# The last feed-forward's gate and up products: Strassen's seven half-size products in place of eight

## The reference, cut to what matters

```
def swiglu_2(a, w13, w2):
    gate, up = jnp.split(a @ w13, 2, axis=-1)
    return (jax.nn.silu(gate) * up) @ w2

f_lat = swiglu_2(modulate(h_lat, m_lat[3], m_lat[4]), ffn_w13[i], ffn_w2[i])
h_lat = layer_norm(DEEPNORM_ALPHA * h_lat + m_lat[5] * f_lat, ln_g[i, 1], ln_b[i, 1])
```

## Time and profile before

| | |
|---|---|
| median of 3 runs | 2859.49 us |
| profiled execution: span from first to last instruction | 2854.2 us |
| what lies around the span (median less span) | 5.3 us |
| PE / DVE / ACT / POOL busy over the span | 99% / 55% / 38% / 19% |
| f4, pairs of parts 2 and 3 (16 pairs) | 87.0 us for each 8 |

### The profile page before, as it was taken

The page is one execution under the profiler, slowest core; times in us unless marked ns, Lnnn a source line. Parts: engine busy times, 40 slices in busy tenths (PEclk is TensorE's granted clock), DMA queues, the critical chain, the costliest instruction groups (busy, mean ns, idle before and its releaser), DMA issues.

```text
span 2854.2 us, 40607 instructions
## 1 busy us (share of the span) xinstructions
PE 2821.6 (99%) x16234; PEld 2449.4 (86%) x16234; DVE 1576.0 (55%) x2738; ACT 1098.0 (38%) x1884; POOL 545.1 (19%) x287
## 2 busy tenths in 40 slices
PE   9999999999999999999999999999999999999998
PEld 8888897988889888888888988888897778988888
DVE  6656588757585543534446743533565636633344
ACT  5322258633234541423324722112235546532222
POOL 2333200033331101111111011111112322122220
PEclk9999999999999999999999999999999999999999
DMA  5544322235553201110211132322422121133231
GB/s 191 166 157 162 119 86 73 68 125 178 164 165 100 75 30 59 52 64 33 67 52 52 45 106 89 118 87 95 137 62 98 54 76 65 53 111 103 96 96 38
DMA packets 85005, 268.85 MB, mean 94 GB/s; under 512 B 9040, under 2 KB 16592, under 8 KB 84432
## 3 DMA queue, kind: packets, MB, share of 16 engines
q1 hardware_dynamic: 84816, 266.25, 28.5%
HBM read 262.54 MB, written 2.10 MB: 93 GB/s over the span
## 4 chain that ended last, share of the span: by engine, by line
PE 95%; DVE 3%; ACT 1%; issue 1%; DMA 0%; SPq 0%; DVEq 0%; ACTq 0%
PE ps L1762 30%; PE ps L1763 30%; PE ps L1764 30%; PE ps L2021 1%; PE ps L2005 1%; PE ps L1994 1%; DMA t_x<-in_x 0%; PE ps L1885 0%; DVE t_m L2403 0%; PE ps L1877 0%; PE ps L1936 0%; DVE t_wlo L2383 0%; PE ps L1893 0%; PE ps L1949 0%; DVE t_m L2465 0%
## 5 line engine op out<-in xcount | busy, mean ns | idle before, releaser
L1762 PE MATMUL ps<-t_h,t_whi 128*128 128x512 f32 (+1 forms) x2320 | 807.0, 348 | 3.5 <-DVE t_wlo L2377 1.3
L1763 PE MATMUL ps<-t_h,t_wlo 128*128 128x512 f32 (+1 forms) x2320 | 802.3, 346 | 0.0
L1764 PE MATMUL ps<-t_h,t_whi 128*128 128x512 f32 (+1 forms) x2320 | 801.6, 346 | 0.0
L2896 POOL TENSOR_TENSOR t_wlo<-t_raw,t_whi 128x1024 fp32r<-128x1024 f32 (+3 forms) x144 | 342.4, 2377 | 1500.7 <-ACT t_whi L2059 1500.7
L2059 ACT CAST t_whi<-t_raw 128x1024 fp32r<-128x1024 f32 (+3 forms) x320 | 320.7, 1003 | 632.3 <-PE ps L1764 592.5
L1762 PEld LDWEIGHTS ps<-t_h,t_whi 128*128 128x128 f32 x2320 | 439.3, 189 | 63.7 <-issue 8.2
L1763 PEld LDWEIGHTS ps<-t_h,t_wlo 128*128 128x128 f32 x2320 | 439.4, 189 | 54.4 <-issue 1.2
L1764 PEld LDWEIGHTS ps<-t_h,t_whi 128*128 128x128 f32 x2320 | 439.1, 189 | 53.9
L1762 PE MATMUL ps<-t_hid,t_whi 128*128 128x256 f32 (+1 forms) x1298 | 421.1, 324 | 0.6 <-DVE t_hid L2530 0.6
L1763 PE MATMUL ps<-t_hid,t_wlo 128*128 128x256 f32 (+1 forms) x1298 | 418.9, 323 | 0.0
L1764 PE MATMUL ps<-t_hid,t_whi 128*128 128x256 f32 (+1 forms) x1298 | 418.3, 322 | 0.0
(11 more groups left out here) (306 smaller groups left out, 4118.5 us busy)
## 6 DMA issues: line engine op xcount, KB each, us to landing
t_raw<-in_gu SPq DMA_DIRECT2D x174, 512.0 KB, 3.3
t_raw<-in_ada SPq DMA_DIRECT2D x96, 512.0 KB, 3.3
t_raw<-in_dn SPq DMA_DIRECT2D x52, 512.0 KB, 3.7
t_raw<-in_dn SPq DMA_DIRECT2D x24, 384.0 KB, 3.2
t_raw<-in_ret_v SPq DMA_DIRECT2D x16, 512.0 KB, 3.3
t_raw<-in_ret_qk SPq DMA_DIRECT2D x16, 512.0 KB, 4.2
t_raw<-in_ret_g SPq DMA_DIRECT2D x16, 512.0 KB, 3.2
t_raw<-in_ret_o SPq DMA_DIRECT2D x16, 512.0 KB, 3.8
```

Source lines behind the costliest of these rows:

```text
L1762: e.matmul(out, whi, xlo, start=first, stop=False, skip_group_check=shared)
L1763: e.matmul(out, wlo, xhi, start=False, stop=False, skip_group_check=shared)
L1764: return e.matmul(out, whi, xhi, start=False, stop=last, skip_group_check=shared)
L2896: e.tensor_tensor(m.block(1, it.slot, n), m.raw(it), m.block(0, it.slot, n), ALU.subtract).then_inc(*S["lo_pool"].of(j))
```

## The change

For 19 of f4's 22 pairs (all but the first three) gate and up are computed together by the Winograd form of Strassen's scheme. The pair is a 2 x 2 matrix of quarters: A11, A12 are gate's weights for the lower and the upper 512 channels, A21, A22 are up's; B11, B12, B21, B22 are the activations, lower or upper channels by first or second 256 tokens. In place of 8 products of quarters there are 7:

- P1 = A11 B11, P2 = A12 B21, P3 = S4 B22, P4 = A22 T4, P5 = S1 T1, P6 = S2 T2, P7 = S3 T3
- sums of weights: S1 = A21 + A22, S2 = S1 - A11 (written as A22 - S3), S3 = A11 - A21, S4 = A12 - S2
- sums of activations, once for all pairs: T1 = B12 - B11, T3 = B22 - B12, T2 = B22 - T1, T4 = B21 - T2 in the kernel's signs.

Each of the seven is 4 steps x 3 matmuls of 256 tokens, with 128 x 512 of weights. PE's order is P1, P2, P6, P5, P7, P3, P4. P6, P7 and P4 go on in P1's PSUM bank after P1, and P3 in P5's; before such a bank is added to, its content is copied to SBUF by ACT (`snap`), or, ahead of P4, taken by DVE (`seven_add` of C22). DVE makes the four results: C11 = P1 + P2, C12 and C22 by one addition each from a copy and a bank, C21 is the bank itself.

POOL makes S3, S1 and S4 of every pair in place in the ring (`wadd`), DVE makes S2 into a spare corner of TMP. ACT copies the seven quarters to hi; POOL writes lo of A12 and S3, DVE of the other five. WHI and WLO are used as eight half slots. A pair's two loads (gate's and up's block) keep their places in the ring until their last sums are split: the first until S3 and S4 are, the second until S1 and A22 are. The activations' sums are made in four chunks c = 0 to 3: POOL adds hi and lo of four quarters (`t_full`), DVE makes T1, T3, T2, T4 one from another (`t_add`), ACT and DVE split them (`t_hi`, `t_lo`); the next chunk's `t_full` waits for this chunk's `t_lo`.

```diff
+QUADS = ("A11", "A12", "S2", "S1", "S3", "S4", "A22")
+HALF = 20
+FULLS = {"T1": 0, "T3": 1, "T4": 2, "T2": 3}
+WADD_POOL = ("S1", "S3", "S4")
+WLO_POOL = ("A12", "S3")
...
+        if slot < NH and known:
+            spare.extend((HALF + 2 * slot + h, after) for h in range(2))
...
+    def assign_half(slot, after):
+
+        j = take_coming()
+        where[j] = slot
+        (pid, srcs), q = known[j]
+        low[j] = "lo_pool" if q in WLO_POOL else "lo_dve"
+        if q == "A11":
+            for which in range(2):
+                put("load", pid=pid, which=which, src=srcs[which])
+        put("prep", j=j, slot=slot, after=after, lo=low[j], q=q, pid=pid)
+        put("prep_lo", j=j)
+        if q == "A12":
+            for name in ("S3", "S1", "S2", "S4"):
+                put("wadd", pid=pid, q=name, old=state["pair"])
+            state["pair"] = pid
...
+                if halves:
+                    for s in range(segs[-1][0] // 256 + 1):
+                        force_tokens(s * 256, 256)
+                    turned_sums(f, ver, halves)
+            if halves:
+                gates, last_h = seven_products(f, ver, gu, [(pi, k, c0 + k) for k in range(size - len(specs) // 2, size)], halves, gates, over_hid, pitch)
...
+    def turned_sums(f, ver, halves):
+
+        after = halves["after"]()
+        for c in range(DC // 2):
+            put("t_full", f=f, ver=ver, c=c, n=halves["n"], after=after)
+            put("t_add", f=f, c=c, n=halves["n"])
+            put("t_hi", f=f, c=c, n=halves["n"], after=after)
+            put("t_lo", f=f, c=c, n=halves["n"])
...
+            banks = {"P1": bank(), "P2": bank(), "P5": bank()}
+            banks.update(P6=banks["P1"], P7=banks["P1"], P4=banks["P1"], P3=banks["P5"])
...
+            product("P1", "A11", "B11", seat(banks["P1"], "drain_dve", (*key, "up", 0)))
+            s1, keys1 = snap("P1")
+            product("P2", "A12", "B21", seat(banks["P2"], "drain_dve", (*key, "C11")))
+            gate1 = gate_slot()
+            add("C11", s1, ids["P2"], banks["P2"], gate1, gates[gate1])
+            free(keys1, ("drain_dve", (*key, "C11")))
+            put("seven_silu", key=(*key, "C11"), slot=gate1, n=n)
+            gates[gate1] = [("drain_dve", (*key, "up", 0))]
+            product("P6", "S2", "T2", [("snap", (*key, "P1"))])
+            s2, keys2 = snap("P6")
+            product("P5", "S1", "T1", seat(banks["P5"], "drain_dve", (*key, "C12")))
+            s5, keys5 = snap("P5")
+            product("P7", "S3", "T3", [("snap", (*key, "P6"))])
+            add("C22", s5, ids["P7"], banks["P7"], None)
+            product("P3", "S4", "B22", [("snap", (*key, "P5"))])
+            gate2 = gate_slot()
+            add("C12", s2, ids["P3"], banks["P3"], gate2, gates[gate2])
+            free(keys2, ("drain_dve", (*key, "C12")))
+            put("seven_silu", key=(*key, "C12"), slot=gate2, n=n)
+            gates[gate2] = [("drain_dve", (*key, "up", 1))]
+            last = product("P4", "A22", "T4", [("drain_dve", (*key, "C22"))])
+            up(0, gate1, None)
+            up(1, gate2, s5)
+            free(keys5, ("drain_dve", (*key, "up", 1)))
...
+                elif old.kind == "load":
+                    for j, lo in old.last:
+                        w.wait_ge("hi", j)
+                        w.wait_ge(lo, j)
...
+    def seven(it):
+        out = m.PS[:, it.bank, 0:it.n]
+        for k in range(4):
+            if k:
+                yield
+            if it.x[0] == "T":
+                w.wait_ge("t_lo", (it.f, it.x, k))
+            else:
+                wait_h(it.ver, (int(it.x[1]) - 1) * 4 + k, (int(it.x[2]) - 1) * it.n, it.n)
+            if k == 0:
+                w.wait_ge(it.lo, it.w)
+                wait_all(it.before)
+            done = products(out, m.weight(0, it.slot, k * P, P), m.weight(1, it.slot, k * P, P), m.factor(it, 0, k), m.factor(it, 1, k),
+                            it.first and k == 0, k == 3, True)
...
+    def wadd(it):
+        if it.q not in WADD_POOL:
+            r1, r2 = it.raws
+            w.wait_ge("wadd_pool", (it.pid, "S3"))
+            w.wait_ge(f"d_ring{r2 % NR}", r2)
+            wait_all(it.taken)
+            e.tensor_tensor(m.quad(r2, "S2"), m.quad(r2, "A22"), m.quad(r1, "S3"), ALU.subtract).then_inc(*S["wadd_dve"].of((it.pid, it.q)))
...
+    def t_add(it):
+        f11, f12, f21, f22 = (m.full(i, it.n) for i in range(4))
+        w.wait_ge("t_sum", (it.f, it.c))
+        e.tensor_tensor(f11, f12, f11, ALU.subtract).then_inc(*S["t_full"].of((it.f, "T1", it.c)))
+        w.wait_ge("t_full", (it.f, "T1", it.c))
+        e.tensor_tensor(f12, f22, f12, ALU.subtract).then_inc(*S["t_full"].of((it.f, "T3", it.c)))
+        w.wait_ge("t_full", (it.f, "T3", it.c))
+        e.tensor_tensor(f22, f22, f11, ALU.subtract).then_inc(*S["t_full"].of((it.f, "T2", it.c)))
+        w.wait_ge("t_full", (it.f, "T2", it.c))
+        e.tensor_tensor(f21, f21, f22, ALU.subtract).then_inc(*S["t_full"].of((it.f, "T4", it.c)))
...
+        r1, r2 = it.raws
+        q11, q12, q21, q22 = m.quad(r1, "A11"), m.quad(r1, "A12"), m.quad(r2, "A21"), m.quad(r2, "A22")
+        if it.q == "S3":
+            w.wait_ge(f"d_ring{r2 % NR}", r2)
+            w.wait_ge("hi", it.pid)
+            w.wait_ge(it.lows["A11"], it.pid)
+            done = e.tensor_tensor(q11, q11, q21, ALU.subtract)
+        elif it.q == "S1":
+            w.wait_ge("wadd_pool", (it.pid, "S3"))
+            done = e.tensor_tensor(q21, q21, q22, ALU.add)
+        else:
+            w.wait_ge("wadd_dve", (it.pid, "S2"))
+            w.wait_ge("hi", it.pid + 1)
+            w.wait_ge(it.lows["A12"], it.pid + 1)
+            done = e.tensor_tensor(q12, q12, m.quad(r1, "S2"), ALU.subtract)
+        done.then_inc(*S["wadd_pool"].of((it.pid, it.q)))
...
+    def t_full(it):
+        n = it.n
+        wait_all(it.after)
+        if it.c:
+            for t in ("T1", "T2", "T3", "T4"):
+                w.wait_ge("t_lo", (it.f, t, it.c - 1))
+        for i in range(4):
+            c, t0 = it.c + i // 2 * 4, i % 2 * n
+            for s in halves(t0, n):
+                w.wait_ge("h_lo", (it.ver, c, s))
+            done = e.tensor_tensor(m.full(i, n), m.h(0, c, t0, n), m.h(1, c, t0, n), ALU.add)
```

231 lines of the change are left out of this document (203 added, 28 removed).

## The result

The changed kernel takes 2882.0 us (median of 4 runs, 2879.0 to 2885.6), the kernel before, run beside it, 2858.8 us (2857.9 to 2861.3). The ratio is 1.0081 with a 95% interval of 1.0068 to 1.0093: 23 us slower, where 2875 us and a range of 2850 to 2892 were forecast. The profiled execution took 2885.6 us, its span is 2883.8 us, 29.6 us more than before's 2854.2. That is more than the 23.2 us between the medians. The profiled execution of the changed kernel was the slowest of its four. That of the kernel before, at 2854.2 us and some 2 us for start and end (1.8 here), is 2 us shorter than any of the three timed ones (2858.0 to 2861.3).

The account below looks back on a forecast made before the run. PE's columns alone were taken to bound the last feed-forward. -15.2 + 22.8 + 6 + 1 + 1 = +15.6 us took the 2854.2 us span to 2869.8; 5.3 us around it made 2875, range 2850 to 2892.

Parts of the forecast that it names:

- waits at weights, 19 pairs: PE's stalls ahead of P7: 13 pairs at 1.5 us and 6 at about 0.5, +22.8 us.
- around it: Instructions the planner moves elsewhere in the kernel: 0, within 2 us either way.
- PE's part: PE's matmuls in f4's pairs: 10.88 us falls to 10.08, 0.80 us less a pair, 15.2 us in 19 pairs.
- The closed chain: POOL's and DVE's turns at SBUF plus the next pair's second load: 11.6 us a pair, PE waiting 1.5 before P7.
- count of pairs: Which of the 19 pairs stall: 13 at 1.5 us and 6 at about 0.5.
- Rival 3: C11 and C22 late too, PE waiting twice a pair: 12.2 us in all 19, +32 us, 2891; chance 12%.
- Rival 4: Weight loads bind, so no PE time saved: 11.0 us a pair, same stalls, 2890; 4% with the rest.
- Rival 1: Weights in stock hide the lag: pairs of 10.1 to 10.5 us, near 2855; chance 25%.
- The first pair: PE waits at P6 for the fourth chunk of T2, whose sums stand behind weights on POOL: 6 us.
- the upper bound I had given (12): First pair's wait if the fourth chunk's POOL sums and DVE instructions each wait out another turn: 12 us.
- The clock: TensorE's clock may halve after the first pair's pause: 0 to 3 us, 1 taken.
- The handovers: Each part's last pair to its down products, waiting for the hidden block's splits: 1 us for three parts.

Follow-up runs that it names:

- e3: Changed kernel with ACT's copy of P6's bank moved ahead of the hi of S2; 2886.5 us, ratio 1.0097 to the kernel before.
- e9: Changed kernel with an unused 512 KB transfer issued ahead of every second load of a pair, from the third pair on; 2908.0 us, ratio 1.0171 to before.
- e5: Changed kernel with POOL's three sums of weights cut to 8 of their 512 columns; 2866.1 us, ratio 1.0027 to the kernel before.
- e1: Changed kernel with a fourth place in the ring of raw weights from the third pair on; 2886.8 us, ratio 1.0104 to the kernel before.
- e4: Changed kernel with ACT's copy of P6 ahead of the hi of S2 and DVE's C22 ahead of the lo of S1; 2886.0 us, ratio 1.0101 to before.
- e6: Changed kernel with eight products again in part 1's three pairs, seven only in parts 2 and 3; 2870.8 us, ratio 1.0046 to the kernel before.
- e8: Changed kernel with the lo of down weights soon after a seven-product block made on DVE, not POOL; 2881.5 us, ratio 1.0081 to before.
- e2: Changed kernel with the lo of A12 and S3 made on DVE, not POOL; 2877.2 us, ratio 1.0066 to the kernel before.

## Why the prediction was right, and where it was off

The direction and the mechanism of the pairs were right. The sum was short by more than its time shows. In spans it gave +15.6 us, and the profiled execution has +29.6: 14 us short, most of it in two terms. That the forecast of 2875 missed the median of 2882 by only 7 is luck: the sum added 5.3 us to get from a span to the median, and for the changed kernel the median lies 1.8 us under the profiled span (2882.0 and 2883.8). Against the sum's own terms, in us of the profiled executions:

| term | forecast | measured |
|---|---|---|
| PE's columns, 19 pairs | -15.2 | -15.2 by 0.120 a matmul |
| waits at weights, 19 pairs | +22.8 | +20.8 in parts 2 and 3, 1.7 in part 1 |
| first pair, activations' sums | +6 | +9.15 in two gaps |
| clock at the first pair | +1 | +3.8, the rest of part 1 |
| handovers to down products | +1 | +8.8 |
| around it | 0 | +0.6 |

The measured 20.8 are the 7.96 us by which parts 2 and 3 grew and the 16 x 0.80 that PE saved in them; 19.8 of them stand as gaps, 1.0 is 16 times the 0.06 us by which a pair's matmuls took longer than 10.08. The 3.8 are what is left of part 1's 12.17 by 3 x 0.80, 9.15 and the gaps of 0.98 and 0.69.

**PE's part** was right to a tenth: the 84 matmuls of a pair take 10.14 us (11.70 less 1.56), which saves 0.74 us a pair and not 0.80.

**The closed chain** was right, and to a tenth: 11.6 to 11.7 forecast and 11.70 measured, the gap 1.5 and 1.56, ahead of P7 and behind ACT's copy, S3 waiting for the load. e3 shows that the wait is the round's and not the copy's, e9 that the load is in it, e5 that POOL's sums are 1.06 us of it. What the prediction didn't have is the second round through PE and DVE's queue, which e1 laid bare: the chain named is the longest of several, and none of its links that was taken away gave its own length back. Its count of pairs was off and did no harm: 13 pairs at 1.5 and 6 at 0.5 were forecast, ten have 1.56, the last pair of part 3 still 1.39, and the first ones of parts 2 and 3 none.

**Rival 3's sum** was too low: 12.2 us in all 19 pairs are 19 x 2.12 = 40 us of stalls and not 36, so that it comes to 2895, over the stated range. No pair of parts 2 and 3 came near it (11.70 at most). Rival 4's was too low as well: 11.0 us a pair with the same stalls is 2893, not 2890.

**Rival 1** (the stock hides it) was wrong for a reason that I hadn't given: in e3 and e4 the stock stays unused while results or copies stand between the weights in a fixed order.

**The first pair** is the first of the two terms that were sized wrong, "It stands 6 us"; it stood 9.15. It had two errors. The fourth chunk's sums began on POOL at 2513.65 and lasted 3.98 us, where I had 2511.5 and 2.9; DVE's part ended at 2522.65 and not at 2517.3: it began behind two of DVE's splits of weights and a lo of a hidden block (1.06, 1.22 and 0.95 us), and two of its four sums waited out POOL's turns (1.15 and 1.37 us in place of 0.42). That is the mechanism of the upper bound I had given (12) and not of the value that I took. And the pair's own S2 was late: DVE made it at 2513.39, behind the third chunk, so PE stood at P6's first matmul already. e6 takes the whole away and gains 10 to 11 us, and some 13 with the 2.4 of PE's gain that it gives up.

**The clock** was taken at 1 us and is 3.8 in the first pair by the rest of part 1 (35 matmuls that stand about 0.21 apart in place of 0.120 make 3.6 of it), and about 1.5 at each of two handovers. This cost isn't fixed: behind the same two pauses e1, e3 and e4 have 21 to 23 such matmuls and lose 2.3 to 2.4 us. The four timed executions of the changed kernel go with that, a granted clock of 0.995 over the whole in the slowest and of 0.996 to 0.997 in the others.

**The handovers** are the other term, "I add 1 us"; they took 8.8, of which 5.8 are the three gaps (0.73, 2.09 and 2.95) and 3.1 the clock behind two of them. The earlier trace rows had shown POOL's 1024 columns in front of such a split with 0.5 us lost. Before, one lo of 512 ended the hidden block; now there are two halves in line, with another weight's split between them, and all of the 2.0 us that POOL holds comes through. e8 bears this out in the profile: 6.1 of the 8.8 us go when the hold goes.

## What to carry to other kernels

Work that is taken off the bounding engine has to be bought from engines that have idle time between waits, and what counts there is not their busy share (over the span 23% for POOL; in four rounds of part 2 DVE 79%, POOL 66%, ACT 55%, and PE waits all the same) but the longest round that their instructions close among themselves, with the load of the next block in it. Follow the round once, then look for the next longest before mending the first: the load taken away gave nothing here, and two of POOL's splits 0.35 us of a round. If a round is a little longer than a pair, apply the change to every second one; that was faster than before here, by 7 us, with 8 of the 22 pairs changed.

## What the runs showed of the hardware

- POOL and DVE take turns at SBUF a whole instruction at a time, also for short ones: a DVE split of 256 columns (0.42 us by itself) lasts 2.48 behind 1024 of POOL's, and S2 of 512 lasts 1.77 beside POOL and 0.68 when POOL's sums are 8 columns long. In turn POOL's 512 columns go from 1.29 to 1.71 and 1.74 us.
- TensorE's clock can fall on short pauses, and the pause's length alone doesn't tell. Half clock (1.2 GHz) was granted from the first of two pauses of 4.41 and 4.74 us on, to 6 us behind the second, and for some 3 us behind one of 2.09. In e1, where PE pauses 1.9 us in each round, one of 1.91 us had 16 matmuls at half clock behind it (2782.4 to 2785.6) and the others of 1.88 to 1.92 had none. In e3 a pause of 2.83 us left the clock full (1.00 from 2682.14 to 2688) and one of 2.94 did not (0.52 from 2820.41 to 2824). Pauses of 0.87 and 1.60 (e8) left it at 1.00. Around 2.5 us it went both ways in e2, where the first row stands behind a pause of 2.62 us and the second behind one of 2.50:

```profile
2678.00:2682.00 4.00, 3.97 (x17) 3.30 (x18) 0.75 (x1) 1.05 (x1) 1.75 (x1) 1.00 0.54 185
2813.40:2817.00 3.60, 3.60 (x15) 3.30 (x16) 0.75 (x1) 1.04 (x1) 0.92 (x1) 0.53 0.00 0
```
